# Squares, sum and root of the first token half moved ahead of the last product of a feed-forward down projection

## The reference

```
def swiglu_ffn(h, w_in, w_out):
    gate, up = jnp.split(h @ w_in, 2, axis=-1)
    return (jax.nn.silu(gate) * up) @ w_out

y = swiglu_ffn(h, ffn_w_in[l], ffn_w_out[l])
x = x + (1.0 + gt2) * rms_norm_2(y, post2_w[l])

# rms_norm_2(x, w) = x * rsqrt(mean(x * x over channels) + 1e-6) * w
```

## Time and profile before

| what | us |
|---|---|
| median of 3 runs (2157.96 to 2159.13) | 2158.52 |
| the profiled execution, its own time | 2156.89 |
| its span, first to last instruction | 2155.2 |
| TensorE busy within the span | 2113.1 |
| mean granted TensorE clock | 0.996 of full speed |

### The profile page before, as it was taken

The page is one execution under the profiler, slowest core; times in us unless marked ns, Lnnn a source line. Parts: engine busy times, 40 slices in busy tenths (PEclk is TensorE's granted clock), DMA queues, the critical chain, the costliest instruction groups (busy, mean ns, idle before and its releaser), DMA issues.

```text
span 2155.2 us, 28843 instructions
## 1 busy us (share of the span) xinstructions
PE 2113.1 (98%) x10931; PEld 1716.0 (80%) x10931; DVE 1254.0 (58%) x1551; ACT 759.4 (35%) x972; POOL 1144.1 (53%) x1036
## 2 busy tenths in 40 slices
PE   7999999999999999999999999999999999999996
PEld 5788887887777878787888888887888888888885
DVE  7988874356652261182469335736585555657486
ACT  6663333334533242112122242224544333332223
POOL 3342224566662323232387344465669888867774
PEclk9999999999999999999999999999999999999998
DMA  6224424232341111111223234342766777766662
GB/s 225 99 98 167 168 76 147 75 102 87 99 146 49 50 59 48 71 49 61 93 92 136 88 127 146 127 176 85 266 233 215 253 253 253 253 246 208 221 214 92
DMA packets 108786, 304.78 MB, mean 141 GB/s; under 512 B 9360, under 2 KB 19856, under 8 KB 108688
## 3 DMA queue, kind: packets, MB, share of 16 engines
q1 hardware_dynamic: 96336, 284.59, 38.1%
q10 hardware_dynamic: 12352, 18.88, 2.4%
HBM read 233.70 MB, written 69.73 MB: 141 GB/s over the span
## 4 chain that ended last, share of the span: by engine, by line
PE 86%; DVE 6%; ACT 3%; DVEq 1%; DMA 1%; issue 1%; POOLq 1%; ACTq 0%; POOL 0%; SPq 0%
PE PG L868 34%; PE PG L874 17%; PE PG L1455 14%; PE PG L1369 6%; PE PX L1478 4%; PE PG L1478 3%; PE PX L1098 1%; PE PX L1093 1%; DVE PX L2298 1%; PE PG L969 1%; DVE UH L3165 1%; DVE WK L2292 1%; PE PX L1076 1%; DMA turn_out<-WK 1%; PE PX L1113 1%
## 5 line engine op out<-in xcount | busy, mean ns | idle before, releaser
L868 PE MATMUL PG<-UL,WH 128*128 128x512 f32 x1696 | 661.2, 390 | 0.0
L868 PE MATMUL PG<-UH,WH 128*128 128x512 f32 x1568 | 625.1, 399 | 4.6 <-ACT WK L2068 1.3
L747 POOL TENSOR_TENSOR TOUCH<-TOUCH 128x2 f32<-128x2 f32 x184 | 55.7, 303 | 828.2 <-PE PG L874 690.6
L750 POOL TENSOR_TENSOR WL<-WRAW,WH 128x1024 fp32r<-128x1024 f32 (+1 forms) x184 | 433.3, 2355 | 30.2 <-issue 30.2
L874 PE MATMUL PG<-UH,WL 128*128 128x512 f32 x1568 | 400.5, 389 | 0.0
L868 PEld LDWEIGHTS PG<-UL,WH 128*128 128x128 f32 x1696 | 318.5, 188 | 67.8 <-issue 3.8
L868 PEld LDWEIGHTS PG<-UH,WH 128*128 128x128 f32 x1568 | 294.3, 188 | 81.0 <-issue 11.2
L874 PEld LDWEIGHTS PG<-UH,WL 128*128 128x128 f32 x1568 | 294.3, 188 | 61.7
L748 POOL TENSOR_SCALAR WH<-WRAW 128x1024 fp32r<-128x1024 f32 (+1 forms) x184 | 190.8, 1037 | 0.0
L1455 PE MATMUL PG<-TH,AH 128*128 128x512 f32 x352 | 137.0, 389 | 0.3 <-POOL AL L796 0.3
L1455 PE MATMUL PG<-TH,AL 128*128 128x512 f32 x352 | 136.9, 389 | 0.0
(11 more groups left out here) (558 smaller groups left out, 3937.3 us busy)
## 6 DMA issues: line engine op xcount, KB each, us to landing
ADA<-ada_w SPq DMA_DIRECT2D x24, 1024.0 KB, 5.9
RAW<-up_w SPq DMA_DIRECT2D x22, 1024.0 KB, 7.7
WRAW<-out_w SPq DMA_DIRECT2D x30, 512.0 KB, 3.7
WRAW<-zg_w SPq DMA_DIRECT2D x24, 512.0 KB, 3.7
gates<-STG ACTq DMA_DIRECT2D x24, 512.0 KB, 2.6
WK<-gates SPq DMA_DIRECT2D x24, 512.0 KB, 3.3
WRAW<-up_w SPq DMA_DIRECT2D x22, 512.0 KB, 3.7
p_gates<-PGB SPq DMA_DIRECT2D x22, 512.0 KB, 2.8
```

The lines of the kernel that those rows point to most:

```text
L747: pool.tensor_tensor(TOUCH[:, 0:2], TOUCH[:, 2:4], TOUCH[:, 4:6], ALU.add)
L750: pool.tensor_tensor(WL[:, r, 0:n], WRAW[:, r, 0:n], WH[:, r, 0:n].bitcast(F32), ALU.subtract).then_inc(w_split, 1)
L868: mm = pe.matmul(out, w[:, r, at + P * k:at + P * k + P], v, start=first and k == ks[0] and n == 0, stop=False)
```

## The change

It does five things, all in the last three sweeps:

1. ACT makes the squares of tiles 4 to 7 of the first half between `b_highs(5)` and `b_highs(6)`, not behind both.
2. DVE adds these four squares (`last_acc(0, 4, KB)`) behind the last `c21_join`, ahead of `b_lows(6)`.
3. PE makes the ones product of the first half behind tile 21 instead of tile 24, and ACT the root behind `b_highs(6)`. The root goes to a buffer of its own, `FIRST_RS`.
4. DVE's list after the joins is reordered: three additions of the second half first, then outputs 0 to 3, one addition, outputs 4 and 5, the fifth addition, outputs 6 and 7.
5. PE waits for both parts of the last `c12_join` ahead of tile 27, where it waited for one ahead of each quarter.

No instruction is added or removed, and no DMA is moved in its queue.

```
@@ PE
-            for n in range(25):
+            for n in range(22):
                 down_op(n)
             pe.wait_ge(norm_acc, 6 + 7)
             pe.matmul(PX[:, 0, :], ONES[:], LAST_ACC, start=True, stop=True).then_inc(norm_ms, 1)
-            for n in range(25, 27):
+            for n in range(22, 27):
                 down_op(n)
             pe.wait_ge(w_split, TILE0["down"] + 28)
+            pe.wait_ge(joined, c22_joined(3) + 2)
             for v in range(2):
-                pe.wait_ge(joined, c22_joined(3) + 1 + v)
                 last_part(v, 0, 3)
@@ ACT
-            for k in (5, 6):
-                for g in range(3):
-                    b_highs(k, g)
+            for g in range(3):
+                b_highs(5, g)
             for j in range(4, KB):
                 act.wait_ge(joined, DOWN_JOINED0 + j + 1)
                 square(0, j, YF[0][:, j, :])
-            half_root(0, LAST_RS)
+            for g in range(3):
+                b_highs(6, g)
+            half_root(0, FIRST_RS)
@@ DVE
+            last_acc(0, 4, KB)
             for p in range(4):
                 b_lows(6, 3 * p, min(3 * p + 3, PAIRS))
                 c22_join(p)
                 dve.drain()
                 c12_join(p)
-            last_acc(0, 4, KB)
...
             dve.wait_ge(x_reloaded, 16 * KB)
             dve.wait_ge(norm_rs, 13)
-            for j in range(KB):
-                y = YF[0][:, j, :]
-                dve.scalar_tensor_tensor(y, y, vec("post2_g", j), LAST_RS, ALU.mult, ALU.mult)
-                dve.drain()
-                dve.tensor_tensor(XR[:, j, half_tok(0)], XR[:, j, half_tok(0)], y, ALU.add).then_inc(norm_lo, 1)
-            last_acc(1, 1, KB - 2)
+            last_acc(1, 1, 4)
+            first_half_out(0, 4)
+            last_acc(1, 4, 5)
+            first_half_out(4, 6)
+            last_acc(1, 5, 6)
+            first_half_out(6, KB)
```

More of the change, by code:

```diff
@@ L439, in square_at @@
         return UHF[:, 4 + j % 2, 512:1024]
+    FIRST_RS = UHF[:, 3, 512:1024]
     LAST_ACC, LAST_RS = UHF[:, 6, 512:1024], UHF[:, 7, 512:1024]
@@ L3353, in _, with first_half_out @@
                 c12_join(p)
-            last_acc(0, 4, KB)
+            def first_half_out(j0, j1):
+                for j in range(j0, j1):
+                    y = YF[0][:, j, :]
+                    dve.scalar_tensor_tensor(y, y, vec("post2_g", j), FIRST_RS, ALU.mult, ALU.mult)
+                    dve.drain()
+                    dve.tensor_tensor(XR[:, j, half_tok(0)], XR[:, j, half_tok(0)], y, ALU.add).then_inc(norm_lo, 1)
             dve.wait_ge(x_reloaded, 16 * KB)
             dve.wait_ge(norm_rs, 13)
-            for j in range(KB):
-                y = YF[0][:, j, :]
-                dve.scalar_tensor_tensor(y, y, vec("post2_g", j), LAST_RS, ALU.mult, ALU.mult)
-                dve.drain()
-                dve.tensor_tensor(XR[:, j, half_tok(0)], XR[:, j, half_tok(0)], y, ALU.add).then_inc(norm_lo, 1)
-            last_acc(1, 1, KB - 2)
+            last_acc(1, 1, 4)
[4 more added lines that the diff above has]
+            first_half_out(6, KB)
             def last_scaled(v, j):
```

## The result

| | before | changed |
|---|---|---|
| median, us | 2158.58 (5 runs) | 2147.68 (5 runs) |
| profiled execution: own time, span | 2156.89, 2155.2 | 2147.68, 2145.9 |
| mean granted clock | 0.996 | 0.998 |

The ratio is 0.9944 with a 95% interval of 0.9932 to 0.9956, so the change saves 10.9 us, 0.5%. One of the five changed executions took 4312.72 us, for which no trace gives a cause; it is left out of the ratio. Measured again later (`h_changed_again`), the same kernel had 2147.47 against 2158.89, ratio 0.9946 (0.9933 to 0.996). The forecast was 2151.2 with a range of 2148.0 to 2154.2: the direction was right, the gain of 7.3 us too small, and the time lies 0.3 us under the range.

What follows compares the result with a forecast made beforehand. TensorE, busy 2113.1 of 2155.2 us, was taken as the bound. With both stalls it restarts 7.3 us sooner, clock and tail adding nothing: 2158.5 - 7.3 = 2151.2 us, range 2148.0 to 2154.2.

Steps and rivals of the forecast that it cites:

- The first stall: Ahead of the first half's ones product, 2.35 us idle: goes; 5.14 us less 0.86 for the product, 4.28 us removed.
- The second stall: Ahead of the second half's sums: shrinks from 5.25 to 2.2 us, TensorE restarting at 2125.1, 7.3 us sooner in all.
- The clock: Behind the last stall, 2.2 us long: the clock falls again, a fall costing 1.6 us, so nothing gained.
- The tail: From ACT's last square to the span's end: 16.3 us, untouched; outputs 6 and 7 covered, cost 0.
- the rival in which only the clock stays up: Behind the shorter last stall the clock doesn't fall: gain 8.9 us, 2149.6; chance 0.25.
- the one in which PE doesn't wait at all: Ahead of the second half's sums, no wait since VectorE is hardly held: gain 11.1 us, 2147.4; chance 0.08.

Runs made afterwards that it cites:

- f_no_hold: The changed kernel with GpSimd's weight splits of tiles 25 to 27 cut to two columns, which leaves work out: 2146.87 us, ratio 0.9948 to before.
- The pair of kernels above: The changed kernel with two extra VectorE additions as tile 25's split begins, both inputs in SBUF or one in PSUM: 2149.25 and 2149.27 us, one run each.
- a_sums_only: The changed kernel with the old order on VectorE, so only the first half's sum is moved: 2154.06 us, ratio 0.9977 to before.
- k_dummies_psum: The changed kernel with two extra VectorE additions, one input in PSUM, as soon as tile 23 is done: 2149.27 us, one run.

## Why the prediction was off, by its steps

**The first stall.** Right. Tile 27 started at 2121.88, in the frame of before 2121.88 - 1.28 = 2120.60; the 4.28 us of the prediction put it at 2120.55. The four additions ended at 2076.20, in that frame 2074.9 (forecast 74.7), and PE didn't wait at tile 22. The root ended at 2089.57, in that frame 2088.3 (2088.2).

**The second stall: the term that was mis-sized.** I put the end of the fifth addition at 2125.0 and had PE restart at 2125.1. It restarted at 2124.65 - 1.28 = 2123.37, 9.0 us sooner than before, not 7.3. The mechanism, VectorE held by each split with one instruction in the gap, was right, and `f_no_hold` shows it; the sizes were wrong. The long form of a split (DWH 1.82, end of tile 25's DWL at 2104.8) was taken for all. In the changed kernel tile 25's was short and ended at 2104.95 - 1.28 = 2103.67, 1.1 us sooner, and the first addition began ahead of its DWL and was not held (0.73 us). So the three additions were through at 2106.28 - 1.28 = 2105.0 where I had 2106.1. And tile 26's DWH, behind a long TOUCH of 0.71, began at 2107.91 - 1.28 = 2106.63 where I had 2106.2. Three instructions of the outputs began ahead of it (the rows from 2106.37 to 2107.80) where I had one. These two instructions, 1.4 us, are what lies between the 2124.7 of my steps and the 2124.60 - 1.28 = 2123.3 that was measured; the rest is that I took 2125.0, a middle value. The hold goes in both directions: in these traces TOUCH and DWH are long where a DVE instruction with two SBUF inputs was under way as they began, and short where DVE waited or had an input in PSUM. The pair of kernels above shows this for TOUCH and DWL (0.69 us in all); for DWH, 1.38 or 1.8 to 1.9, it rests on the rows alone. The 0.86 us by which the ones product delays PE had moved the end of `b_lows(6)` into the split of tile 24, so that DVE was waiting for PE (0.73 us, at 2099.64) when tile 25's split began. I had shifted POOL by the 0.86 and left its durations alone.

**The clock.** The price of a fall was right, 1.6 us, except where the low clock outlasts the restart for longer (1.9 in `a_sums_only`), and the doubt whether 2.2 us would bring one was right too. Since the stall was 0.46 us and not 2.2, the fall didn't come: from the restart to the last square are 2129.62 - 2124.65 = 4.97 us, where before had 2138.91 - 2132.39 = 6.52, 1.55 less. 9.02 + 1.55 = 10.57, which is the 10.58 of the last stretch. Had the stall been 2.2, the forecast of a fall would have been a matter of chance: at 1.84 us it came in three executions of ten (by their mean clock), at 2.07 it did not in the one there was, and at 2.34 and 2.35 it came in both traces that had one.

**The tail.** Right: 16.28 against 16.3, and outputs 6 and 7 ended at 2127.63, under PE's sums.

**Range and rivals.** The time lies between the rival in which only the clock stays up (2149.6) and the one in which PE doesn't wait at all (2147.4), close to the latter. I had treated the end of the addition and the clock as separate terms, but an addition that comes 1.7 us sooner also saves the clock. The case with both I gave only to VectorE not being held at all, at 0.08, and let the range end just above it.

## What to carry to other kernels

Where a stall is shortened, the slow clock behind it may go too, and in these runs it came behind no stall up to 1.57 us, behind some of 1.84 to 2.07, and behind every one in the traces from 2.34 on; the two gains belong in one case with one chance. Where two engines hold each other, a shift of one by less than a microsecond changes both engines' durations, so the order of events has to be worked out again and not shifted. And an off-path chain (here squares, additions, root) is best put where both its engines are seen idle in the trace: behind the last `c21_join` it cost TensorE no more than the product itself (0.86 us), and 5.14 us where it was.

## What the runs showed of the hardware

- With a stall of TensorE of 0.44 to 0.46 us the granted clock stayed at 2.4 GHz in all nine executions (by their mean clock, two of them by a trace); with 1.55 it stayed in the one there was (`k_dummies_psum`), as it did in all twelve traces behind the stall of 1.50 to 1.57 near 554 us; with 1.84 and 1.86 it came down to 1.2 GHz in three of ten (two by a trace); with 2.07 it stayed in the one there was; with 2.34 and 2.35 it fell in both traces; with 3.29 it fell in all six (one by a trace).
- In seven of the eight falls behind such stalls in the traces, the clock was at 0.50 for some 3.3 us, beginning between 0.2 us ahead of the restart and 1.4 us after it, and at different products in two traces of the same kernel. Behind the stall of 5.10 in `a_sums_only` the clock was low for some 6.8 us, 2.9 of them ahead of the restart.
- GpSimd's tiny TOUCH (128x2) took 0.20 us, or up to 0.73 when VectorE was in an instruction with two SBUF inputs. VectorE's addition of 0.69 took up to 3.71 beside a split, its joins with one input in PSUM not more than 0.70.
